# A block of two model layers on one core: input products of two turns of the state space loop in one go, other shares of weight steps, and the v columns read out by ScalarE

## The reference

```python
h = rms_norm(x, norm1_w[l], RMS_EPS)
z = h @ w_in[l]                                   # u | q | k | v | gs | ga
# s5_mixer, 64 groups of 16 channels, 64 complex states each
bu_r = jnp.einsum('blgc,gpc->blgp', ug, bb_r)     # input products
bu_i = jnp.einsum('blgc,gpc->blgp', ug, bb_i)
_, _, s_r, s_i = lax.associative_scan(combine, (a_r, a_i, bu_r, bu_i), axis=1)
y = einsum(s_r, c_re) - einsum(s_i, c_im) + d_skip * ug
y = jax.nn.gelu(y); y_ssm = y * jax.nn.sigmoid(y @ w_glu + b_glu)
# diff_attention: rms_norm of q and k, two softmaxes per head, their difference times v
m = (sigmoid(z[..., o_gs:o_ga]) * (y_ssm @ w_proj_ssm[l])
     + sigmoid(z[..., o_ga:]) * (y_attn @ w_proj_attn[l]))
```

## Time and profile before

| | |
|---|---|
| median of three runs | 2373.97 us |
| the profiled execution | 2377.31 us |
| its span in the profile | 2375.5 us |
| PE busy | 2321.3 us (98%) |
| DVE busy | 1480.4 us (62%) |
| ACT busy | 1174.3 us (49%) |
| granted clock of PE, mean | 0.993 |
| the loop of 16 turns | about 68 to 308 us of the span |

### The profile page before, as it was taken

How to read it: one execution, slowest core, us unless ns; L and a number is a source line. 1 busy time by engine, 2 the same in 40 slices (tenths; PEclk the granted TensorE clock), 3 DMA queues, 4 the chain that set the end, 5 groups by cost and what they waited for, 6 DMA issues and landing times.

```text
span 2375.5 us, 35851 instructions
## 1 busy us (share of the span) xinstructions
PE 2321.3 (98%) x14863; PEld 1938.5 (82%) x14863; DVE 1480.4 (62%) x1854; ACT 1174.3 (49%) x1651; POOL 188.7 (8%) x210
## 2 busy tenths in 40 slices
PE   8999999999999999999999999999999999999998
PEld 8777777888888888888888898878888888788886
DVE  5999956756555554444444446846765558457667
ACT  5676656644554444444443444634564546335643
POOL 5000000002000000000000001030100010301043
PEclk9999999999999999999999999999999999999999
DMA  9544565565666666666666676434746665337566
GB/s 258 177 153 153 163 195 154 152 198 183 186 188 188 185 193 186 191 190 186 193 189 192 188 225 188 133 100 113 192 133 215 184 195 152 103 99 187 142 216 204
DMA packets 305860, 416.92 MB, mean 176 GB/s; under 512 B 52937, under 2 KB 164105, under 8 KB 304929
## 3 DMA queue, kind: packets, MB, share of 16 engines
q1 hardware_dynamic: 299232, 395.63, 56.3%
q0 software_dynamic: 6144, 18.91, 2.6%
q10 hardware_dynamic: 320, 0.08, 0.0%
HBM read 406.94 MB, written 7.87 MB: 175 GB/s over the span
## 4 chain that ended last, share of the span: by engine, by line
PE 84%; DVE 10%; ACT 3%; issue 2%; DMA 0%; POOLq 0%; SPq 0%; ACTq 0%; DVEq 0%; POOL 0%
PE banks L657 82%; DVE wp_hl L1240 3%; ACT wp_hl L1982 2%; PE banks L772 1%; DVE r_SA L1800 0%; PE banks L784 0%; DMA xt<-x 0%; DVE u_z L1592 0%; PE banks L901 0%; DVE nsd L1655 0%; ACT L1982 0%; DVE xt L1285 0%; DVE xt L1282 0%; PE banks L882 0%; DVE xt L1280 0%
## 5 line engine op out<-in xcount | busy, mean ns | idle before, releaser
L1240 DVE TENSOR_TENSOR wp_hl<-raw,wp_hl 128x1024 fp32r<-128x1024 f32 x740 | 916.0, 1244 | 813.0 <-ACT wp_hl L1982 812.1
L1982 ACT ACTIVATE wp_hl<-raw 128x1024 fp32r<-128x1024 f32 x740 | 782.4, 1060 | 1020.9 <-PE banks L657 997.5
L657 PE MATMUL banks<-wp_hl,XX_hl 128*128 128x512 f32 x3840 | 899.1, 393 | 6.4 <-DVE wp_hl L1240 6.3
L657 PEld LDWEIGHTS banks<-wp_hl,XX_hl 128*128 128x128 f32 x3840 | 718.3, 189 | 167.7 <-issue 11.0
L657 PE MATMUL banks<-XX_hl,wp_hl 128*128 128x256 f32 (+1 forms) x3584 | 631.6, 332 | 2.1 <-DVE XX_hl L1240 1.2
L657 PEld LDWEIGHTS banks<-XX_hl,wp_hl 128*128 128x128 f32 x3584 | 526.5, 190 | 72.2 <-issue 11.9
L657 PE MATMUL banks<-wp_hl,FF_hl 128*128 128x512 f32 x1056 | 240.6, 389 | 0.0
L657 PEld LDWEIGHTS banks<-wp_hl,FF_hl 128*128 128x128 f32 x1056 | 197.9, 188 | 40.9
L657 PE MATMUL banks<-wp_hl,MXa_hl 128*128 128x512 f32 x384 | 88.4, 389 | 0.0
L657 PE MATMUL banks<-wp_hl,MM_hl 128*128 128x512 f32 x384 | 88.3, 390 | 0.0
L657 PEld LDWEIGHTS banks<-wp_hl,MXa_hl 128*128 128x128 f32 x384 | 72.0, 188 | 15.1
(11 more groups left out here) (471 smaller groups left out, 1795.5 us busy)
## 6 DMA issues: line engine op xcount, KB each, us to landing
raw<-w_in SPq DMA_DIRECT2D x304, 512.0 KB, 3.9
raw<-w_out SPq DMA_DIRECT2D x96, 512.0 KB, 4.1
raw<-w_ffn_gate SPq DMA_DIRECT2D x88, 512.0 KB, 3.7
raw<-w_ffn_up SPq DMA_DIRECT2D x88, 512.0 KB, 3.7
raw<-w_ffn_down SPq DMA_DIRECT2D x88, 512.0 KB, 4.0
raw<-w_proj_attn SPq DMA_DIRECT2D x16, 512.0 KB, 4.9
raw<-w_proj_ssm SPq DMA_DIRECT2D x16, 512.0 KB, 4.9
raw<-w_uq SPq DMA_DIRECT2D x24, 256.0 KB, 4.1
```

The lines of the kernel that those rows point to most:

```text
L657: return e.matmul(o, lhsT, rhs, start=start, stop=stop, skip_group_check=True)
L1240: return tt(d, src, hi, SUB)
L1982: return e.activation(o, x, func, bias=bias, scale=scale)
```

## The change

Four things, in the diff below.

1. The input products of two turns are made together, in every second turn: four row tiles of 32 rows write banks 4, 5, 6 and 7. DVE reads banks 4 and 5 in the even turn, 6 and 7 in the odd one.
2. Banks 6 and 7 are thereby no longer free for the result and the transposed weights. These use banks 4 and 5, so they wait until DVE has read the even turn's products (`ROT z`).
3. The shares in the loop are 4.5 steps in place of 4.3 on all three engines.
4. Both banks of `v0` and `v1` are read out by ACT.

```diff
-    cols("v", 2, w1, 3072, 16, "AV", tokens=True)
+    cols("v", 2, w1, 3072, 16, "AA", tokens=True)
...
         def s_weights(i):
-            bank(7, *WT("w", i))
+            bank(5, *WT("w", i))
...
         def s_result(i):
-            bank(6, *YV("y", i))
+            bank(4, *YV("y", i))
...
-            e.wait_ge(*WT("w", i))
-            bank(4, *ROT("z", t))
-            bank(5, *ROT("z", t))
-            for part in range(2):
-                for k in range(2):
-                    rows = slice(32 * (r + k), 32 * (r + k) + 32)
-                    last = mm(B[4 + k][:, 256 * part:256 * part + 256], BT[i % 2][rows, 128 * part:128 * part + 128], uT[rows, i, :],
-                              part == 0, part == 1)
-            last.then_inc(BPJ.made("b", t), 1)
-            main(at.share(4.3))
-            if t and r == 0:
+            if t % 2 == 0:
+                e.wait_ge(*WT("w", i))
+                for k in range(4):
+                    bank(4 + k, *ROT("z", t + k // 2))
+                for part in range(2):
+                    for k in range(4):
+                        rows = slice(32 * k, 32 * k + 32)
+                        last = mm(B[4 + k][:, 256 * part:256 * part + 256], BT[i % 2][rows, 128 * part:128 * part + 128], uT[rows, i, :],
+                                  part == 0, part == 1)
+                last.then_inc(BPJ.made("b", i), 1)
+            main(at.share(4.5))
+            if t and t % 2 == 0:
                 s_result(i - 1)
...
-            e.wait_ge(*BPJ("b", t))
+            e.wait_ge(*BPJ("b", t // 2))
+            o = 2048 + 1024 * (t % 2)
...
-            elif n == "v":
-                c = int(l)
-                ts(vM[:, 1, 512 * c:512 * c + 512], b[1], rs[:, 3:4], None, MUL).then_inc(s_evV, 1)
...
-                act(vM[:, 0, 512 * c:512 * c + 512], b[0], ACT.Identity, scale=rs[:, 2:3]).then_inc(s_evA, 1)
+                for i in range(2):
+                    act(vM[:, i, 512 * c:512 * c + 512], b[i], ACT.Identity, scale=rs[:, 2 + i:3 + i]).then_inc(s_evA, 1)
```

More of the change, by code:

```diff
@@ L834, in s_weights @@
         def s_weights(i):
-            bank(7, *WT("w", i))
+            bank(5, *WT("w", i))
             e.wait_ge(*SV("bp"))
             e.wait_ge(*SSP("x"))
[L838 to L841, removed]
+            e.transpose(B[5][:, 0:128], BP[0][:, 128 * i:128 * i + 128], ident)
+            e.transpose(B[5][:, 128:256], BP[1][:, 128 * i:128 * i + 128], ident)
+            e.transpose(B[5][:, 256:384], X1[:, i, :], ident)
+            e.transpose(B[5][:, 384:512], X2[:, i, :], ident).then_inc(WTR.made("t", i), 1)
         def s_result(i):
-            bank(6, *YV("y", i))
+            bank(4, *YV("y", i))
             e.wait_ge(*SCN("co", 2 * i + 1))
@@ L848, in s_result @@
                     c, o = 32 * n, 512 * (n % 2) + 256 * part
-                    last = mm(B[6][c:c + 32, 0:256], CT[i % 2][:, w, c:c + 32], turns[(2 * i + n // 2) % 4][x][:, o:o + 256], m == 0, m == 3)
+                    last = mm(B[4][c:c + 32, 0:256], CT[i % 2][:, w, c:c + 32], turns[(2 * i + n // 2) % 4][x][:, o:o + 256], m == 0, m == 3)
             last.then_inc(CPJ.made("c", i), 1)
@@ L853, in _ @@
         for t in range(16):
-            i, r = t // 2, 2 * (t % 2)
+            i = t // 2
             if t == 0:
                 emptied(e, "u1")
-            e.wait_ge(*WT("w", i))
-            bank(4, *ROT("z", t))
-            bank(5, *ROT("z", t))
-            for part in range(2):
-                for k in range(2):
-                    rows = slice(32 * (r + k), 32 * (r + k) + 32)
-                    last = mm(B[4 + k][:, 256 * part:256 * part + 256], BT[i % 2][rows, 128 * part:128 * part + 128], uT[rows, i, :],
-                              part == 0, part == 1)
-            last.then_inc(BPJ.made("b", t), 1)
-            main(at.share(4.3))
-            if t and r == 0:
+            if t % 2 == 0:
[10 more added lines that the diff above has]
+            if t and t % 2 == 0:
                 s_result(i - 1)
-            if r == 0 and i < 7:
+            if t % 2 == 0 and i < 7:
                 s_weights(i + 1)
-            main(at.share(4.3))
+            main(at.share(4.5))
         main(at.go(4))
@@ L1299, in evac @@
             b = [B[x] for x in j.banks]
-            if n not in ("gs", "ga", "glu") and n[:2] != "fg" and j.name not in HALF:
+            if n not in ("v", "gs", "ga", "glu") and n[:2] != "fg" and j.name not in HALF:
                 e.wait_ge(*over(j.name))
@@ L1550, in s_result @@
                 e.wait_ge(*CPJ("c", i))
-                stt(out=yT[:, i, :], in0=uT[:, i, :], scalar=col("ssmd", i), in1=B[6][:, 0:256], op0=MUL, op1=ADD).then_inc(YV.made("y", i), 1)
+                stt(out=yT[:, i, :], in0=uT[:, i, :], scalar=col("ssmd", i), in1=B[4][:, 0:256], op0=MUL, op1=ADD).then_inc(YV.made("y", i), 1)
         four = lambda a: a.rearrange("p (k r t) -> p k r t", k=2, r=2)
@@ L1560, in _ @@
             e.wait_ge(*TA("co", t))
-            e.wait_ge(*BPJ("b", t))
+            e.wait_ge(*BPJ("b", t // 2))
+            o = 2048 + 1024 * (t % 2)
             if t > 3:
                 e.wait_ge(*CPJ("c", t // 2 - 2))
-            tt(four(zi_), frames("co"), four(banks[:, 2048:3072]), MUL)
-            tt(four(u["z"]), frames("si"), four(banks[:, 2048:3072]), MUL).then_inc(ROT.made("z", t), 1)
+            tt(four(zi_), frames("co"), four(banks[:, o:o + 1024]), MUL)
+            tt(four(u["z"]), frames("si"), four(banks[:, o:o + 1024]), MUL).then_inc(ROT.made("z", t), 1)
             e.wait_ge(*ROT("z", t))
@@ L2211, in s_weights @@
                 e.wait_ge(*CPJ("c", i - 2))
-            act(BT[i % 2], B[7][:, 0:256], ACT.Copy)
-            act(ct[:, 0:256], B[7][:, 256:512], ACT.Copy)
-            act(ct[:, 256:384], B[7][:, 256:384], ACT.Copy, scale=-1.0).then_inc(WT.made("w", i), 1)
+            act(BT[i % 2], B[5][:, 0:256], ACT.Copy)
+            act(ct[:, 0:256], B[5][:, 256:512], ACT.Copy)
+            act(ct[:, 256:384], B[5][:, 256:384], ACT.Copy, scale=-1.0).then_inc(WT.made("w", i), 1)
         s_weights(0)
```

## The result

| | before | changed |
|---|---|---|
| median of 10 runs each, us | 2374.74 | 2381.95 |
| lowest to highest, us | 2373.53 to 2377.42 | 2380.30 to 2383.57 |
| profiled execution (span), us | 2377.31 (2375.5) | 2381.66 (2379.8) |

The ratio is 1.0031, with an interval of 1.0023 to 1.0039. The change makes the kernel 7.2 us slower. The forecast was 2371.3 us in a range that ended at 2380. It had the sign wrong, and the time lies outside the range.

The account below looks back on a forecast made before the run. PE and DVE were both taken as full in the loop, balanced to about 1%, with PE the bound after it. Terms -7.7 + 1.0 + 0.8 - 2.6 + 5.8 = -2.7 us gave a median of 2371.3 us, range 2364 to 2380.

Parts of the forecast that it names:

- Part 1, the products: In the loop: sixteen products become eight with four row tiles side by side, so PE loses 10.0 us of work.
- Rival 3: The four row tiles do not run abreast and PE's 10.0 us stay: +4.0 us, 2378.0 us; chance 0.05.
- Part 2, the work of DVE: In the loop, DVE has four more splits, +4.5 us, and no v columns, about 1.3 us less.
- Part 2, the waits of DVE: DVE's waits on ACT and PE, 8.1 us in all, shrink with a lighter PE; 1.4 us taken off.
- signs of being wrong: Listed beforehand: products taking twice as long, new waits of DVE inside the loop, or glu running through without a stall.
- part 2: Loop shares: last result starts at 300.8 in place of 305.84, two steps more done: -7.7 us (-11 to -2.5).
- the slow rival: In the loop, banks tie PE and DVE, DVE waits about 1 us a pair: +5.3 us, 2379.3 us; chance 0.12.
- The slow clock behind the last result: At the loop's end, a lower clock after PE's stalls around the last result: +1.0 us (0 to 1.6).
- Part 3, the tie: In the loop, result and weight transposes wait for the even turn's rotation: nothing more added.
- Part 4, gs3 and ga1: Sigmoids one piece earlier: gs3 between the first two exponentials +0.8 us; ga1 leaving u = 2, -2.6 us (-4 to 0).
- Part 4, glu: Sigmoids of ga3 ahead of the last square root: PE stalls 4.2 us, slow clock 1.6: +5.8 us (3 to 8).

Follow-up runs that it names:

- d1: The changed kernel with one glu piece (two steps on DVE and ACT) moved ahead of the four splits of aT: 2372.99 us, ratio 0.9994 to before.
- a1: The kernel before with shares of 4.5 steps in place of 4.3, nothing else: 2384.45 us, ratio 1.0036 to before.
- a2: The kernel before with two turns' products in one group and the banks that go with it, shares still 4.3: 2375.63 us, ratio 0.9997 to before.
- a3: The kernel before with both halves of v read out by ACT, nothing else: 2376.46 us, ratio 1.0005 to before.
- a4: The changed kernel with shares of 4.3 steps in place of 4.5: 2371.81 us, ratio 0.9985 to before.
- a5: The changed kernel with its loop ended two steps lower, at step 174, on PE, DVE and ACT, shares still 4.5: 2380.22 us, ratio 1.0020 to before.
- c1: The kernel before with PE's result also waiting for DVE's rotation of the next even turn: 2374.87 us, ratio 1.0004 to before.
- c2: The changed kernel with shorter q and k read-outs on ACT, two squares per tile in place of eight: 2376.12 us, ratio 1.0003 to before.
- e0_before: The kernel before, unedited, profiled a second time: 2374.83 us for that execution.

## Why the prediction was wrong

One measure separates work from waiting in the loop. I took the time from DVE's first rotation to the end of its last turn back, and subtracted DVE's idle stretches over 0.15 us in it. The last column says for how many us the clock was low around the first products, because of the wait near 77 us (see d1):

| kernel | length, us | idle | work | low clock |
|---|---|---|---|---|
| before (second profile) | 228.35 (228.58) | 4.57 (4.91) | 223.78 (223.67) | 6.8 (6.8) |
| changed | 236.93 | 9.89 | 227.04 | 6.8 |
| a1, shares alone | 241.16 | 12.76 | 228.40 | 6.8 |
| a2, products alone | 225.04 | 1.71 | 223.33 | 3.4 |
| a3, v alone | 226.29 | 3.90 | 222.39 | 3.4 |
| a4, changed with 4.3 | 224.80 | 2.83 | 221.97 | 6.8 |
| a5, changed, loop to 174 | 235.48 | 8.36 | 227.12 | 3.4 |
| c1, tie alone | 227.37 | 3.63 | 223.74 | 3.4 |
| c2, short read-outs | 232.93 | 5.87 | 227.06 | 6.8 |
| d1, one piece moved | 235.35 | 8.28 | 227.07 | 3.4 |

- **Part 1, the products: right.** The profile has eight groups of 16 records, 1.15 us each but for the first at low clock. From the start of a product to the next matmul, all groups took 18.2 us before and 9.6 after; with eight times the 0.19 us of switching gone too, that is about 10 us, as predicted. Rival 3 falls. What ended the saving was not the reading of the banks (DVE's two rotations take 1.2 us each, as before) but DVE's waits for ACT's copies.
- **Part 2, the work of DVE: right.** Predicted were four splits more and v less, or +4.5 - 1.3 = +3.2 us. The table has 227.04 - 223.78 = +3.3. That PE ends up waiting for DVE was right too.
- **Part 2, the waits of DVE: this is the step that failed.** The prediction says of the waits on ACT and PE that they "shrink with a lighter PE; I take 1.4 us off". They grew by 5.3 us (4.57 to 9.89). A lighter PE does shorten them, by 1.7 to 1.9 us when profiles of the same low clock are compared (a4's 2.83 with 4.57, a2's 1.71 with c1's 3.63), so the 1.4 is no bad size for that. But the shares move the read-outs against the copies, and that costs more: a1 has 12.76, and c2, with the read-outs of q and k shortened, is back at 5.87. I looked at how many steps a share has and not at which of ACT's long instructions stand ahead of a copy of the same share. With 4.3 no split was behind the first q read-out in its share; with 4.5 there is one. The order of instructions on ACT would have shown this, and the 4 us of a q read-out could have been read off the trace of before. New waits of DVE inside the loop were one of the prediction's own signs of being wrong. The last result so starts 2.65 us later, with two steps more done (2.7 us): part 2 is worth -0.1 where I had -7.7. It also lies outside my bounds of -11 to -2.5. I had 306 as the upper end of the last result and wrote "new waits, see the slow rival" without sizing any. The lower end, 297.5, counted on most of the 8.1 us of waits, of which only 4.57 lay where they could bring the result forward.
- **The slow clock behind the last result: wrong, small.** The waits were 1.43 and 1.63 us, and no low clock followed. +1.0 was put there, 0 came.
- **Part 3, the tie: right.** c1 and a2 show it to cost nothing.
- **Part 4, gs3 and ga1: stalls right.** The stall behind `S0` is 0.59 (0.8 predicted), the one at u = 2 is 1.29 (1.4 predicted). From the start of `S0` to the last sum before the sigmoids the kernel took 116.90 us before and 114.90 after: -2.0, with -1.8 predicted. That the total fits is partly luck. In the second profile of before the same stretch took 115.32 us, so against that one only 0.4 us are gained. And the length of a wait alone doesn't keep the low clock away, as I had supposed for the shorter wait at u = 2: in the profile that I worked from, the wait of 1.78 us at `S0` was followed by one at 336 us, which I had not seen.
- **Part 4, glu: mechanism and stall right, the clock behind it too small.** The stall is 4.11 us (4.2 predicted). My working has a slip in it: T + 9.9 with 1.4, 0.7 and 1.1 is T + 13.1 and not 13.4, which makes a stall of 3.9 us. The four splits then held DVE's weight split up for 2.4 us (461.33 to 463.74) and not 2.1, which hides the slip. The stage grew by 30.70 - 23.03 = 7.67 us, so the low clock costs 3.56 and not 1.6. I had taken the price of a stretch that followed a stall of 2.60 us, where the clock was low for 3.4 us; here it was low for 6.8.
- **The sum.** By profiles -0.1, -2.0 and +7.7 make +5.6, where the difference is 4.35. The rest is in three places: the wait behind the last result is shorter (1.63 for 1.99: -0.4); the two steps that stood between the last sum and `glu` took 454.68 - 451.49 = 3.19 us before and nothing now, which is 0.4 more than I count for them; and -0.4 comes behind `glu`. Set against my sum of -2.7, part 2 accounts for 7.6 us of the error and `glu` for 1.9. The medians differ by more, 7.2 us. The profile that I worked from stood 2.6 us over its median, with low clocks at 336 and 411 us that another execution of the same kernel doesn't show (e0_before). The gain at u = 2 counted one of them, 1.4 us, as if every execution had it.

Not settled: a2 and a4 have the same loop (last result at 302.61 and 302.87), and the same waits behind it, yet their medians differ by 3.8 us. Their profiles are 2.4 us apart. A low clock of 3.4 us at 407 in that of a2, absent in that of a4, is 1.4 us of it, and behind `glu`, where the low clock near 1870 us lasts 10.2 us in a2 and 6.8 in a4, it is another 1.1. Whether v on ACT makes such stretches less frequent was not tried. Nor was a version with 4.5 in which only the order of read-outs and copies on ACT is changed.

## What to carry to other kernels

When two engines in a loop laid out by hand are both full, taking work from one buys only what the other gives back. Here 10 us less on PE alone brought the last result forward by 3.2 us in the profile and left the median where it was. With v moved too, the last result came at the same time and the median was 3.9 us lower, for a reason that isn't settled. Before changing how much filler goes into a gap, list for the third engine, which looked half idle, what its long in-order pieces stand in front of: ACT, 69% busy in the loop, decided both the waits in the loop and the stall in `glu`. And a stall is to be priced with the clock behind it, which here nearly doubled it.

## What was not expected of the hardware

Four row tiles of 32 rows side by side take 1.15 us for 16 records, two take 1.13 for 8. After a stall of 4.11 us the clock was low for 6.8 us and 3.56 us were lost; after one of 4.18 us (a5) it was low for 10.2 us; after the same 2.60 us wait it was low for 3.4 us in one profile of the kernel before and not at all in the other. Shorter waits do not keep it away for certain either. After the wait of 1.78 us at `S0` it was low for 3.4 us in one profile of before (at 336) and not in the other, and after the 1.99 us behind the last result it was low for 3.4 us in a3 (at 308.7) and not in either profile of before.
